# Differential attention with 64-row scores and an earlier rotary and gate, and expert weight tiles with four neighbouring rows in each partition

## What is computed

```python
def diff_attend(q, k, v, lam):                 # q, k: (.., 4 heads, 2, tokens, 64), v: (.., 128)
    s = einsum("bhiqd,bhikd->bhiqk", q, k) * (64 ** -0.5)
    p = softmax(s, axis=-1)
    a = p[:, :, 0] - lam * p[:, :, 1]
    return einsum("bhqk,bhkd->bhqd", a, v)

q = apply_axial_rope(qk_heads(da_q), cos, sin)
k_all = concatenate([k_ctx, apply_axial_rope(qk_heads(da_k), cos, sin)], axis=3)
out_da = merge_heads(rmsnorm(o_da, da_subln) * (1.0 - lambda_init))
out_hg = merge_heads(rmsnorm(o_hg_lat, hg_norm)) * silu(hg_g)
y_lat = concatenate([out_da, out_hg], axis=-1) @ w_out

def expert_choice_ffn(h, w_router, w_gate, w_up, w_down):   # 16 experts, 32 tokens each
    aff = softmax(h @ w_router); top_aff, top_idx = top_k(aff.T, 32)
    xin = h[top_idx]
    y = (silu(xin @ w_gate[e]) * (xin @ w_up[e])) @ w_down[e] * top_aff    # each w: 1024 x 1024
    return scatter_add(y, top_idx)
```

## Time and profile before

| | us |
|---|---|
| median of 3 runs (1234.88 to 1236.12) | 1235.96 |
| the profiled execution | 1234.43 |
| its span, first to last instruction | 1232.6 |
| TensorE busy | 952.2 (77%) |
| VectorE busy | 316.0 (26%) |
| ScalarE busy | 213.6 (17%) |
| GpSimd busy | 46.8 (4%) |

### The profile page before, as it was taken

One profiled execution on the slowest core, in us unless ns is written; L12 is line 12 of the kernel. 1 busy time (PEld: TensorE's weight loads), 2 busy tenths in 40 slices (PEclk: granted clock), 3 DMA queues, 4 the chain that ended last, 5 costly groups with the idle time before them and its releaser, 6 DMA issues.

```text
span 1232.6 us, 11054 instructions
## 1 busy us (share of the span) xinstructions
PE 952.2 (77%) x4392; PEld 479.9 (39%) x4392; DVE 316.0 (26%) x579; ACT 213.6 (17%) x431; POOL 46.8 (4%) x98
## 2 busy tenths in 40 slices
PE   4799989998887769666666655555566998989987
PEld 2666455745344344111111111111113854534843
DVE  1398253624751243000000000000003124421002
ACT  2123131212351212000000000000002033311010
POOL 0200000001000100000000000000001000000000
PEclk9899989998898969888888888888887999998999
DMA  9934352845558619999999999999997441032000
GB/s 355 339 139 141 132 205 86 302 158 205 172 198 308 265 41 389 407 409 410 410 409 410 410 410 410 409 410 410 410 410 287 158 154 69 1 112 93 1 1 34
DMA packets 102231, 310.46 MB, mean 252 GB/s; under 512 B 2705, under 2 KB 4932, under 8 KB 102068
## 3 DMA queue, kind: packets, MB, share of 16 engines
q1 hardware_dynamic: 99700, 301.04, 63.4%
q0 software_dynamic: 2496, 8.93, 2.2%
HBM read 308.91 MB, written 1.05 MB: 251 GB/s over the span
## 4 chain that ended last, share of the span: by engine, by line
PE 57%; DMA 29%; DVE 6%; SPq 3%; issue 2%; ACT 1%; POOL 1%; POOLq 0%; DVEq 0%; ACTq 0%
PE bank L768 40%; DMA ring<-w_up_dram 25%; PE bank L1100 7%; PE bank L786 3%; SPq L661 2%; DMA ring<-w_ada_dram 2%; DMA ring<-w_down_dram 2%; PE bank L776 1%; PE bank L897 1%; PE bank L982 1%; PE bank L796 1%; SPq L646 1%; PE bank L1232 1%; PE bank L1255 1%; PE bank L1131 1%
## 5 line engine op out<-in xcount | busy, mean ns | idle before, releaser
L1100 PE MATMUL bank<-ring,ilat 128*32 128x512 f32 x960 | 149.3, 779 | 122.1 <-DMA ring<-w_up_dram 122.1
L1100 PEld LDWEIGHTS bank<-ring,ilat 128*32 128x32 f32 x960 | 36.7, 139 | 233.4 <-issue 154.7
L768 PE MATMUL bank<-ring,hT 128*128 128x512 f32 x224 | 102.0, 616 | 3.7 <-DVE gates L1911 2.0
L768 PE MATMUL bank<-ring,kT 128*128 128x512 f32 (+1 forms) x224 | 99.5, 606 | 5.2 <-DVE kT L1677 3.4
L2106 DVE TENSOR_TENSOR state<-state,bank 64x512 f32<-64x512 f32 x16 | 11.0, 689 | 345.4 <-ACT state L1547 345.4
L768 PE MATMUL bank<-hT,ring 128*128 128x256 f32 (+1 forms) x320 | 86.6, 431 | 3.6 <-DVE hT L1715 3.6
L1118 PE MATMUL bank<-ring,ilat 128*32 128x512 f32 x512 | 61.1, 598 | 16.2 <-ACT ilat L1551 11.6
L768 PEld LDWEIGHTS bank<-hT,ring 128*128 128x128 f32 x320 | 61.7, 195 | 28.4 <-issue 17.7
L1547 ACT ACTIVATE state<-bank 64x512 f32<-64x512 f32 x16 | 9.5, 591 | 349.7 <-PE bank L1100 349.7
L768 PEld LDWEIGHTS bank<-ring,hT 128*128 128x128 f32 x224 | 43.9, 198 | 59.2 <-issue 57.3
L768 PEld LDWEIGHTS bank<-ring,kT 128*128 128x128 f32 x224 | 43.8, 197 | 59.3 <-issue 59.3
(11 more groups left out here) (321 smaller groups left out, 1021.8 us busy)
## 6 DMA issues: line engine op xcount, KB each, us to landing
ring<-w_down_dram SPq DMA_DIRECT2D x32, 2048.0 KB, 23.8
ring<-w_gate_dram SPq DMA_DIRECT2D x32, 2048.0 KB, 20.1
ring<-w_up_dram SPq DMA_DIRECT2D x32, 2048.0 KB, 23.7
ring<-w_ada_dram SPq DMA_DIRECT2D x24, 2048.0 KB, 11.7
ring<-w_in_dram SPq DMA_DIRECT2D x8, 2048.0 KB, 12.5
ring<-fno_w_in_dram SPq DMA_DIRECT2D x4, 2048.0 KB, 8.2
ring<-w_out_dram SPq DMA_DIRECT2D x2, 2048.0 KB, 15.3
ring<-mla_w_in_dram SPq DMA_DIRECT2D x2, 2048.0 KB, 21.5
```

Of the source, the lines that this page charges most:

```text
L768: ins = pe.matmul(o, l, r, start=start and i == 0, stop=stop and i == len(terms) - 1)
L1100: ins = pe.matmul(bank[0][32 * t:32 * t + 32, :], x[:, j, :], w[2 * half + t // 2][:, j % JH, n0:n0 + TN], start=j == 0, stop=j == J - 1)
```

## The change

**Experts.** A half is laid out so that partition `p` holds the four neighbouring rows 4p to 4p + 3, one closed piece of 16 KB. The contraction then runs over another order of the rows, and the other operand must follow: `spread(x)[:, g, j, :]` takes columns 4q + j of half g, every fourth element, as the 128 columns of a chunk. It is used in the transposes ahead of the router, in the gathering of tokens, in the transposes of the hidden rows and in the modulation columns of the FFN; the router's weights, the FFN's norm weights and its biases are stored in the same order.

**Mixer.** The rotary and the output gate stand right behind the last level, ahead of the values. Queries and keys are turned in place, and a score contracts over 64 partitions, the two maps of a head in partitions 0 to 63 and 64 to 127; `qz` and its clearing are gone. The first two heads' scores stand ahead of the cross products. The gate is z * (tanh(z/2) + 1) * 0.5 * `hg_norm`, made before the recurrent output, which is then normalised and multiplied with it in one operation (`recurrent_out`, in the loop's first turn). The difference is no longer divided by the first sum: a = p0 + p1 * (lambda * s0 / s1), and since the norm behind it removes a factor s0, only its eps is scaled, by s0 squared (`eps_sums`). One reduction takes both maxima, over two banks. GpSimd loads `ctx_2` and makes its root earlier, and issues three DMAs ahead of the root of the recurrent output.

**Slots.** `kvctx` goes to slot 4 and is requested when the recurrent output is done; the other tiles share slots 0 to 3 without it. Tile 7 comes ahead of tile 2.

```diff
+def spread(x):
+    return x.rearrange("p (h q j) -> p h j q", q=P, j=4)
...
-        for t in (3, None, 4, None, 6, None, 5, None, None, 1, None, None, 0, None, None, None, None, 2, None, 7):
+        for t in (3, None, 4, None, 6, None, 5, None, None, 1, None, None, 0, None, None, None, None, 7, 2, None):
...
-        for i, (name, _) in enumerate(stream):
-            place(name, i % EARLY_SLOTS)
+        for name, _ in stream:
+            if name[0] == "kvctx":
+                place(name, EARLY_SLOTS)
+            else:
+                place(name, turn % EARLY_SLOTS)
+                turn += 1
...
         def expert_src(w, e, half):
-            return w[bass.ds(e, 1), half * TN:(half + 1) * TN, :].rearrange("e (j p) n -> p (e j) n", p=P)
+            return w[bass.ds(e, 1), half * TN:(half + 1) * TN, :].rearrange("e (p j) n -> p (e j n)", p=P)
...
-            for i, (name, src) in enumerate(stream):
-                if i >= EARLY_SLOTS:
-                    wait_filled(sp, last_reader(stream[i - EARLY_SLOTS][0]))
+            for name, src in stream:
                 s = slot_of[name]
+                if name[0] == "kvctx":
+                    wait_filled(sp, ("oh", TB - 1))
+                elif turn_of[name]:
+                    wait_filled(sp, last_reader(occupants[s][turn_of[name] - 1]))
...
             wait_filled(pool, ("oh", TB - 1))
             for i, n in enumerate(("norm_post_mix", "norm_post_ffn")):
                 pool.dma_start(post_norm[i][:, :], a[n][0].partition_broadcast(P)).then_inc(sem("post_in"), 16)
-            pool.dma_start(c2, a["ctx_2"][0].rearrange("(b p) d -> p b d", p=P)).then_inc(sem("ctx2_in"), 16)
+            pool.dma_start(router4, a["w_router"][0].rearrange("(h p j) e -> p h j e", p=P, j=4)).then_inc(sem("router_in"), 16)
             root_inverse(0, TB * HEADS, "rstd_oh")
...
-                    ins = pe.transpose(o[:, jj * P:(jj + 1) * P], src[:, j * P:(j + 1) * P], ident)
+                    chunk = spread(src)[:, g, jj, :] if interleaved else src[:, j * P:(j + 1) * P]
+                    ins = pe.transpose(o[:, jj * P:(jj + 1) * P], chunk, ident)
...
+            def da_scores(b, h):
+                o = [pe_take(pe, ("s", b, h, i)) for i in range(2)]
+                for i in range(2):
+                    ps = slice(64 * i, 64 * i + 64)
+                    fills(pe.matmul(o[i][:, :], q3[ps, h, b * P:(b + 1) * P], k3[ps, h, :],
+                                    start=True, stop=True), ("s", b, h, i))
...
-            def da_scores(b, h):
-                for i in range(2):
-                    o = pe_take(pe, ("s", b, h, i))
-                    fills(pe.matmul(o[:, :], qz[i][:, h * T + b * P:h * T + (b + 1) * P], k3[:, h, :],
-                                    start=True, stop=True), ("s", b, h, i))
...
-                                 [(xn[:, b, j * P:(j + 1) * P], onehot2[:, b, 0:EA * CAP]) for b in range(TB)])
+                                 [(spread(xn[:, b, :])[:, g, jj, :], onehot2[:, b, 0:EA * CAP]) for b in range(TB)])
...
-                c = (2 * n) % 4
-                step(dve.reciprocal(cf[:, c:c + 2], rs[:, c:c + 2]))
+                c = 2 * (n % 2)
+                step(dve.reciprocal(cf[:, c:c + 1], da_sums[:, 8 + n:9 + n]))
                 st.settle()
-                step(dve.tensor_tensor(cf[:, 4 + c:5 + c], cf[:, c + 1:c + 2], lamc, ALU.mult))
+                step(dve.scalar_tensor_tensor(cf[:, c + 1:c + 2], cf[:, c:c + 1], da_sums[:, n:n + 1], lamc,
+                                              ALU.mult, ALU.mult))
                 st.settle()
-                step(dve.tensor_scalar(pbuf[c + 1], pbuf[c + 1], cf[:, 4 + c:5 + c], None, ALU.mult))
-                st.settle()
-                step(dve.scalar_tensor_tensor(pbuf[c], pbuf[c], cf[:, c:c + 1], pbuf[c + 1], ALU.mult, ALU.add),
+                step(dve.scalar_tensor_tensor(pbuf[c], pbuf[c + 1], cf[:, c + 1:c + 2], pbuf[c], ALU.mult, ALU.add),
                      "a_ready")
...
-            output_gate(0)
             da_max(0)
             da_max(1)
             da_difference(0)
...
                 if n == 0:
-                    output_gate(1)
+                    recurrent_out()
```

268 lines of the change are left out of this document (146 added, 122 removed).

## The result

The changed kernel takes 1203.62 us in the median of four runs (1199.85 to 1206.12), the kernel before on the same chip 1236.04: a ratio of 0.973, with a 95% interval of 0.970 to 0.975. The profiled execution took 1199.85 us (span 1198.0), 34.6 less than that of before. The forecast was 1195; the time lies in the range, 8.6 us above the forecast. The stream's 19 us came out at 18.3; the experts, forecast to start 21 us earlier, start 14.5 us earlier (443.51 in place of 458.02), and 4.4 of the missing 6.5 are weight loads with a stride. The profiled execution was forecast at 1194.4, so 5.4 us of the miss can be looked for in the trace. The rest is the step from it to the median: the execution is the fastest of the four, 3.8 us under their median, where the forecast allowed 1.5 (and 1194.4 + 1.5 is 1195.9, not the 1195 that was written).

A forecast was written before the change was run, and what follows sets the result against it. TensorE or its waits bound the mixer and routing, weight loading the sixteen experts. Stream 19 us plus mixer and loop 21 (10.3 + 4.3 + 4.0 + 3.4, 1 off) gave 40 us less: 1195 us median, range 1184 to 1214.

The forecast's parts named there:

- The stream: Experts' weight tiles: 16-KB pieces run at 430 GB/s in place of 410, 19 us less over experts 2 to 15.
- a ceiling: Rival on the experts' weights: 16-KB pieces run like 8-KB ones, near 423 GB/s; 1202 us; chance 0.16.
- pieces that don't grow: Rival on the experts' weights: the queue cuts rows at 4 KB, stream unchanged, only 21 us left; 1214 us; chance 0.08.
- Strided weight loads: FFN operands on TensorE, every fourth element: loads hide behind products, cost taken as zero, at most 10 us.
- strides at twice the time: Rival on TensorE's FFN operands: strided weight loads take twice the time; 1205 us; chance 0.10.
- Rotary and gate ahead: Mixer: rotary and gate ahead of the values; first product with values at 312.4 instead of 322.70, 10.3 us earlier.
- No idle of TensorE at the rotary products: Sign expected in the mixer's profile after: the idle times of 3.15 and 2.01 us gone.
- The recurrent output: Loop's start: VectorE's eight small operations (2.2 us) wait for the root but stay hidden; 2 to 4 us if late.
- queues that are late: Rival in the mixer: SyncE's or GpSimd's queue is late and half the mixer's gain is spent; 1206 us; chance 0.06.
- The loop: Loop over eight block-heads: sigmoid 4.3, context weights' slot 4.0, scores 3.4, with 1 off for new waits; 10.7 in the table.
- the sigmoid: Loop's second turn: the gate's sigmoid, with its 3.35-us reciprocal, leaves VectorE; 4.3 us less.
- the end of the loop behind the last modulation tile: Context weights leave the ring, so the last tile is requested three turns earlier; 4.0 us less.

The follow-up runs named there:

- kernel 3: Changed kernel with expert tiles as two 8-KB pieces per partition instead of one of 16 KB, operands every second element; 1203.45 us, ratio 0.973.
- kernel 6: Changed kernel with ScalarE's copy of modulation 10, VectorE's recurrent output and GpSimd's root for it issued earlier; 1198.91 us, ratio 0.970.
- 7: Changed kernel with only ScalarE's copy of modulation 10 put ahead of the exponentials that wait for VectorE; 1201.09 us, ratio 0.972.
- base: The changed kernel as it is, against the kernel before; 1203.62 us, ratio 0.973; run again 1204.58 us, ratio 0.974.
- kernel 4: Changed kernel with the context weights back in the ring of four slots, in their turn; 1207.86 us, ratio 0.978.
- Kernel 8: Changed kernel with TensorE's strided operands outside the experts' loop made contiguous, plus kernel 6's three moves; 1193.62 us (0.965), again 1191.86 us (0.963).

## Why the prediction was right, and where it was off

- **The stream (19 us).** Right, and for its reason. The law of a fixed cost per piece, read from three rows of before, gave 430 GB/s; 16-KB pieces run at 429. Its 8-KB row, 423 GB/s over only 2 us, is borne out too: 422 over 360 us (kernel 3). The rivals of a ceiling and of pieces that don't grow are out. The Trainium skill ("DMA: Bandwidth & Descriptors", "Why small descriptors are slow (HBM only)") gives a fixed cost of about 3 cycles per packet, from which the step from 4 to 16 KB is worth some 1.7%, an estimate from that page's figure. The traces disagree: it is worth 429/410, 4.6%, and there the measurement decides.
- **Strided weight loads (0 us).** This is the first step that failed. The prediction bounded them by 10 us and took zero, "because these loads hide behind products now". Where the product is long, most of a load does hide. The FFN's modulation columns are products of two columns, which leave next to nothing to hide a load behind (324 ns each, where the contiguous ones take 192), and they were 3.4 of the 4.7 us. The rival of strides at twice the time had the mechanism, with 0.10. It was too large since the transposes (1.97 us for 8 before, 1.98 after; the other 8 took 1.04 and 1.12) and the gathering of the other experts (5.43 and 5.55 us a half) hid theirs. The 1.3 us of the first gathering are the least certain part: with contiguous operands it took 5.52 to 6.41 us in the runs, so it may be 2. The Trainium skill's rule of 16-byte lines ("SBUF — State Buffer", "Door 1: The DMA port swizzle") fits that far: elements 16 bytes apart double the time of a small product, elements 8 bytes apart don't. No run here tells lines from distance as such.
- **Rotary and gate ahead (10.3 us).** The sum is right: the first product with values was forecast at 312.4, and came at 315.42 with 3.1 us of strides ahead of it. Two errors cancel in it. "No idle of TensorE at the rotary products" was wrong, by 2.12 us: ScalarE's copy, which frees the bank, stood behind two exponentials that waited for VectorE, and kernels 6 and 7 took the wait away. And the two pairs of scores were put in at their old price of 3.4 us and took 1.92, since their gain had been booked in the loop.
- **The recurrent output (0 us, "2 to 4 us if the root is late").** The second step that failed. It was seen that what stands behind VectorE's eight operations is needed at about 321. Not seen was that these hold the bank of product 0, at about 317.5, and that they stand behind two others in VectorE's order. That makes 4.32 us from the first product with values to modulation product 0, in place of 0.98, and the product itself runs at the lower clock (3.57 us up to the next piece in place of 1.86): 5.1 us up to the second turn. The rival of queues that are late named GpSimd's three DMAs. They are worth 0.3 us of it: in base the root was there 1.5 us before its reader, and VectorE's order was the larger part of what kernel 6 could move. What is left, 2.52 us in place of 0.98, is the root and VectorE's eight operations themselves.
- **The loop (10.7 us).** It gave 12.3 although the gathering lost 1.3. Piece by piece, against before: the second turn is 3.9 us shorter (4.3 forecast for the sigmoid, which was not tried apart); the end of the loop behind the last modulation tile 5.5 us (4.0 forecast; kernel 4 gives 5.7); three other turns 1.4 us together. The 2.9 us that are left were not forecast at all: the wait at the end of the first block "stays", it said, and it fell from 2.94 us with a product at the lower clock (3.46) to 0.86 and 1.42 with one at the higher clock (1.92). No kernel here tries that apart.
- **The sum.** Strides 4.4 (by the table), product 0 5.1, the loop 2.9 better than forecast, the experts 0.7 worse, the first stretch 0.1 and what lies behind the experts 1.8 better: 5.4 us, which is 1199.85 - 1194.4. The 1.8 us are chance, and the loop's 2.9 came by a way that the forecast did not know, so the total is nearer than its terms. Kernel 8 mends the strides and takes the rotary's wait away, but only part of the second failed step: from the first product with values to the second turn it takes 5.8 to 5.9 us, in place of base's 7.9 and before's 2.8. That its medians of 1192 to 1194 us lie where the forecast was is in part luck.

## What to carry to other kernels

Cost a strided operand where the product is shortest, not where most of its bytes are: here the loads hid behind the long products only, and a layout of every second element gave back on TensorE what it lost on the queue. When work moves ahead, list for every bank and buffer who frees it and what stands in front of that instruction on its own engine; "needed by" is set by the bank's next user too. And where a variant measures the same, read its rows before saying that the cause is absent: two effects of 5 to 6 us cancelled here. The same holds for a sum that comes out right: look at its terms.

## What the runs showed of the hardware beyond that

- Rate of a saturated queue by size of piece: 2 KB 386, 4 KB 410, 8 KB 422, 16 KB 429 GB/s. 4 to 8 KB saves 0.069 us per MB, 8 to 16 KB 0.039: nearly halves each time.
- Two products that contract over 64 rows each, in different halves of the array and into different banks, take 0.55 of the time of two in the same half (1.06 against 1.91 us a pair, both at a granted clock of 1.00).
- The modulation product at 30 us and the columns behind it, which stand behind a wait for a transfer, run at either clock from one execution to the next, in code that no edit touches. The chain of base, and that of kernel 8 the second time:

```profile
30.28 1.92 PE bank L813 x16
```

```profile
30.54 3.64 PE bank L813 x16
```

The columns behind it take 1.89 and 3.52 us. Together these 3.4 us are most of the 4 by which the common start moves from one profiled execution to another, which is why such executions are compared from there on. They may be much of the spread of the other runs too (1199.85 to 1206.12 for base), of which no rows exist.
